# Two placement changes in a fused two-block transformer kernel: when GpSimd norms the residual stream, and when a mixer's convolution rows are turned

## The chip, the cores and the metric

The kernel runs on one core of one Trainium2 chip. The metric is the device time of one execution in microseconds (us), median over runs. A change below about 0.2% of it (3.3 us) can't be told from none.

## The reference

The input is a sequence of 256 tokens with 1024 features, in float32. Two blocks follow one another, each of two layers.

```python
def first_block(x, ...):
    for i in range(DEPTH):                       # 2 layers
        h = rmsnorm(x, norm_mix[i])
        x = x + (mixer_even if i % 2 == 0 else mixer_odd)(h, ...)
        x = x + ec_moe(rmsnorm(x, norm_ffn[i]), ...)      # 16 experts
    return rmsnorm(x, final_norm)                # gain "final_norm"

def second_block(x, ...):
    h = x
    for layer in range(DEPTH):                   # 2 layers
        h = h + 0.5 * _swiglu(_rmsnorm(h, norm_ffn1[layer]), ...)   # 1024 -> 2816 -> 1024
        hn = _rmsnorm(h, norm_mix[layer])
        h = h + (_attn_conv_mixer if layer % 2 == 0 else _recurrent_mixer)(hn, ...)
        h = h + 0.5 * _swiglu(_rmsnorm(h, norm_ffn2[layer]), ...)
    return _rmsnorm(h, norm_final)

def _attn_conv_mixer(h, ...):                    # "the third mixer"
    ...
    attn = _swa_sink_attention(q, k, v, sinks, rel_bias)
    glu = u[..., o3:o4] * jax.nn.sigmoid(u[..., o4:])
    c = jax.nn.silu(_layernorm(_causal_depthwise_conv(glu, conv_w, conv_b), ln_g, ln_b))
    return jnp.concatenate([attn, c], axis=-1) @ w_out
```

Between the blocks stands `rmsnorm(x, final_norm)`. Its result is both the input of the first feed-forward of the second block and the residual stream that this feed-forward is added to.

## The kernel before

The program is written engine by engine, and every engine works through its own list in the order in which the code issues it. Semaphores are the only thing that ties the engines together, so the order around the change is the order of the code.

**Units.** Weights come from memory in slots of 128 x 4096 float32 (2048 KB) into a ring of six. A slot holds four units of 128 x 1024. Each unit is split in two before TensorE uses it: ScalarE copies it, rounded, into `unit_hi` (`split_high`, L548), and VectorE subtracts that from the original into `unit_lo` (`split_low`, L553). There are four buffers of either, so the high part of unit u is written once TensorE has used unit u-4. Activations are split in the same way (`hT_hi` and `cat_lo`, `near_both`, `act_hi` and `act_lo`), and TensorE computes high x high, low x high and high x low.

**Feed-forward `ffn0`.** It is worked off in 22 tiles of 128 hidden features. A tile f has a gate unit, an up unit and a down unit. TensorE computes gate and up (L2004, L2005 with the high part, L2008 with the low one; in the first tile L2019, L2020, L2026), VectorE scales them by the row norms (`scaled`, L2145), ScalarE takes the silu (L2115), and VectorE multiplies (`product`: L2154, L2155, and L2157, which raises the semaphore `ffn_act`). TensorE then runs the down unit of tile f (L2082) behind gate and up of tile f+1, so product f has the time of two hidden matmul groups to be ready. On VectorE a tile is: low part of the next gate unit, scale gate, low part of the next up unit, scale up, product, low part of the down unit.

**Norming the stream.** The second block's first feed-forward reads the rows of x as they came out of the experts; the norm between the blocks is folded into its scales. The stream itself must still be normed before `ffn0` is added to it. That is `restore_pool` on GpSimd: two multiplications of 128 x 1024 by the gain row (L1115) and two by the rows' scale (L1118). It waits for the scale (`power_out`) and for the last transposes that read the raw x (`turned`). VectorE waits for its signal (`x_ready` 3) only after the 22nd tile. GpSimd has nothing else to do until the next norm.

**The third mixer's output projection `s_out`.** The concatenated row has 1024 features: the first 512 from attention, the last 512 from the convolution. The projection has eight units (c, j), c the half of the output columns and j the pair of 128-feature blocks of the input, in the order of `MIXED_UNITS`: (0,0), (0,1), (1,0), (1,1), (0,2), (0,3), (1,2), (1,3). The first four need attention alone, the others the convolution rows. The convolution, done by VectorE, ends about when attention does. Its layer norm's statistics follow (`norm_conv`), and VectorE signals the normed rows with `ln_done` (L2408). TensorE turns these rows, 8 transposes in two groups of four (`turn_pe(pe, "cat_s")`, L430), ScalarE takes the silu out of the two banks (`conv_silu`, L2318) and makes the high part (L2323), and VectorE makes the low part (`conv_low`, L2415). Unit (0,2), the fifth, waits for that. A table load for silu stands ahead of L2318 on ScalarE.

Numbering the units 0 to 7, TensorE's order before is units 0, 1, 2, 3, turn, units 4 to 7 (L2273 with the high parts, L2279 with the low ones). ScalarE splits units 0 to 3, runs `conv_silu`, then splits 4 to 7 and two units of the next feed-forward. VectorE splits units 0 and 1 inside `norm_conv`, then 2 and 3, then makes the low parts of the rows, then splits 4 to 7. The eighth unit is interleaved with the residual's additions (L787) and the next norm.

Of the kernel before, what the change touches and what calls it, by code (L numbers as in the profile page):

```python
# [70 lines left out]
def build(nc, stream, ahead, params, consts, buckets, final_rows, x_in, out):  # L71
    ctx = ExitStack()
    with ctx:
# [3 lines left out]
        def sem(name):  # L77
            return ctx.enter_context(nc.semaphore(name))
# [21 lines left out]
        def pc(name):  # L100
            return par[:, PCOL[name][0]:PCOL[name][1]]
# [102 lines left out]
        ffn_act = sem("ffn_act")  # L204
# [24 lines left out]
        def ge(eng, s, v):  # L229

            if v > 0:
                eng.wait_ge(s, v)
# [8 lines left out]
        def used(eng, n):  # L241

            eng.wait_ge(slot_used[n % RING], n // RING + 1)
# [176 lines left out]
        def turn_pe(pe, name, lo=0, hi=None):  # L420
            first, end = TURN_AT[name]
            for g in range(first + lo, end if hi is None else first + hi):
                if g >= 4:
                    pe.wait_ge(*TURN_DONE[g - 4])
                for src, at, rows, cols in TURNS[g][0]:
                    out = bank[g % 4][0:rows, at:at + cols]
                    if name == "s1" and g == end - 1:
                        last = nc.tensor.matmul(out, src, flip, start=True, stop=True)
                    else:
                        last = nc.tensor.transpose(out, src, ident)  # L430
                last.then_inc(turned, 1)
# [98 lines left out]
        def high_buf(name, u):  # L530
            if name in ("r_in", "r_out"):
                return rec_units[(u + (16 if name == "r_out" else 0)) % 3][0][:, :]
            return unit_hi[:, buffer(name, u), :]

        def low_buf(name, u):
            if name in ("r_in", "r_out"):
                return rec_units[(u + (16 if name == "r_out" else 0)) % 3][1][:, :]
            return unit_lo[:, buffer(name, u), :]
# [440 lines left out]
        rows, rows_sq = W[:, 0:D], W[:, 2048:2048 + D]  # L979
        x_sq = [W[:, 1024:1536], W[:, 1536:2048], W[:, 4096:4608], W[:, 4608:5120]]  # L980
        ZX, ZZ, ZM, ZR = 80, 84, 88, 104

        def quarter_ready(eng, p, i):

            eng.wait_ge(*(PARTS[p][i] if i < 3 else X_SOURCE[p]))
# [125 lines left out]
        def restore_pool(pool):  # L1111
            pool.wait_ge(power_out, POWERS["f0"] + 1)
            pool.wait_ge(turned, TURN_AT["n4"][1])
            for t in range(NT):
                nc.gpsimd.tensor_tensor(x[:, t, :], x[:, t, :], rows, ALU.mult).then_inc(weighted, 1)  # L1115
            pool.wait_ge(weighted, NT)
            for t in range(NT):
                last = nc.gpsimd.tensor_scalar(x[:, t, :], x[:, t, :], stat[:, ZR + t:ZR + t + 1], None, ALU.mult)  # L1118
            last.then_inc(x_ready, 1)
# [1075 lines left out]


        conv_bank = [bank[0], bank[1]]
        convw = pc("convw").rearrange("p (c j) -> p c j", c=4)

        OPS = [(c, j) for c in range(4) for j in range(KW + 1)]  # L2200
# [2 lines left out]
        def s_mix_pe(pe):  # L2203
# [41 lines left out]
            for u, (c, j) in enumerate(MIXED_UNITS):  # L2245
                high = high_buf("s_out", u).rearrange("p (k c) -> p k c", k=2)
                low = low_buf("s_out", u).rearrange("p (k c) -> p k c", k=2)
                if u == 4:
                    pe.wait_ge(ln_done, 1)
                    turn_pe(pe, "cat_s")  # L2250
                if c == 0:
                    left_ready(pe, "s_out", j)
                if j == 0:
                    for t in range(NT):
                        ge(pe, proj_free[t], freed(first + c - 2, t))
                high_ready(pe, "s_out", u)
                if (c, j) == MIXED_UNITS[-1]:
                    low_ready(pe, "s_out", u)
                    for t in range(NT):
                        for kk in range(2):  # L2260
                            for left, right in ((hT_hi, high), (cat_lo, high), (hT_hi, low)):
                                mm = nc.tensor.matmul(proj_bank(first + c, t)[:, :], left[:, 2 * j + kk, t * P:(t + 1) * P],
                                                      right[:, kk, :], start=False, stop=(kk == 1 and right is low),
                                                      skip_group_check=True)
                        mm.then_inc(unit_used if t else tail_done, 1)
                        if t == 0:
                            raw_turn_pe(pe, "n6", 0)
                            raw_turn_pe(pe, "n6", 1)
                    break
                for kk in range(2):  # L2270
                    for t in range(NT):
                        for left in (hT_hi, cat_lo):
                            nc.tensor.matmul(proj_bank(first + c, t)[:, :], left[:, 2 * j + kk, t * P:(t + 1) * P],  # L2273
                                             high[:, kk, :], start=(j == 0 and kk == 0 and left is hT_hi), stop=False,
                                             skip_group_check=True)
                low_ready(pe, "s_out", u)
                for kk in range(2):
                    for t in range(NT):
                        mm = nc.tensor.matmul(proj_bank(first + c, t)[:, :], hT_hi[:, 2 * j + kk, t * P:(t + 1) * P],  # L2279
                                              low[:, kk, :], start=False, stop=(j == 3 and kk == 1), skip_group_check=True)  # L2280
                mm.then_inc(unit_used, 1)

        def s_mix_act(act):
            n0 = START["s_in"]

            def gate(c):
                if c % 2 == 0:
                    act.wait_ge(wide_done, 1 + c // 2)
                else:
                    used(act, n0 + c // 2)  # L2290
                ge(act, wide_dve, c - 1)
                nc.scalar.activation(gate_s[:, c % 2, :], bank[4 + c][:, T:2 * T], ACT.Sigmoid).then_inc(wide_act, 1)

            gate(0)
            act.wait_ge(spread_ready, 1)
            act.dma_start(spread.ap(), spread_sb).then_inc(spread_out, 16)
            gate(1)
            act.wait_ge(spread_out, 16)
            for t in range(NT):
                src = bass.AP(tensor=spread, offset=1 + P * t, ap=[[1, P], [SPAN, S_HEADS], [1, T]])  # L2300
                act.dma_start(bias_s[:, :, t * T:(t + 1) * T], src).then_inc(rows_in, 16)
            gate(2)
            gate(3)
            for m in range(*PROJ_AT["s_in"]):
                for t in range(NT):
                    proj_copy_one(act, m, t, (uS[:, t, 0:512], uS[:, t, 512:768])[m - PROJ_AT["s_in"][0]], scalar=True)
            act.wait_ge(v_turned, 1)
            nc.scalar.activation(vS[:, :, :].rearrange("p a b -> p (a b)"), bank[7][:, 0:T], ACT.Copy).then_inc(v_out, 1)
            turn_evac(act, 0, "s1")
            attend_act(act, "s")  # L2310

            def conv_silu():
                for j in (2, 3):
                    g = TURN_AT["cat_s"][0] + j - 2
                    act.wait_ge(turned, g + 1)
                    for kk in range(2):
                        c = 2 * j - 4 + kk
                        last = nc.scalar.activation(silu_s[:, c, :], bank[g % 4][:, kk * T:(kk + 1) * T], ACT.Silu,  # L2318
                                                    bias=pc("lnb")[:, c:c + 1], scale=pc("lng")[:, c:c + 1])
                    last.then_inc(silu_done, 1)  # L2320
                for j in (2, 3):
                    act.wait_ge(silu_done, j - 1)
                    nc.scalar.activation(hT_hi[:, 2 * j:2 * j + 2, :], silu_s[:, 2 * j - 4:2 * j - 2, :],  # L2323
                                         ACT.Copy).then_inc(turn_hi, 1)

            for u in range(4):
                split_high(act, "s_out", u)
            conv_silu()
            for u in range(4, 8):
                split_high(act, "s_out", u)  # L2330
            for u in range(EARLY):
                split_high(act, "ffn1", u)

        def s_mix_dve(v):
# [48 lines left out]
            between = [107, 114, 120, 126, 128]  # L2383
            attend_dve(v, "s", lambda i: taps(between[i], between[i + 1]), first=lambda: taps(103, between[0]))
            norm_conv(v)
            for u in range(2, 4):
                split_low(v, "s_out", u)
            for j in (2, 3):
                conv_low(v, j)
            for u in range(4, 8):  # L2390
                split_low(v, "s_out", u)
            ahead_low(v, "ffn1")
            residual_add(v, "s_out")
# [579 lines left out]
```

## Time and profile before

| | us |
|---|---|
| median of 3 runs | 1632.93 (1632.87 to 1633.9) |
| span of the profiled execution | 1628.0 |
| TensorE matmul busy in the span | 1435.8 |
| VectorE busy | 942.5 |
| ScalarE busy | 614.5 |
| GpSimd busy | 41.6 |

The profiled execution is given by its span, from the first to the last instruction; no time of its own is listed beside it. The median lies 4.9 us above the span, for what is around the instructions. Times in the rows are positions in the span. PE is TensorE's matmul, PEld its weight load, DVE VectorE, ACT ScalarE, POOL GpSimd. A timeline row has the start, the duration, the engine, the line, the operation, output<-inputs, the shape, and in brackets the idle time ahead of it and who ended it.

### The profile page before, as it was taken

To read this page: it belongs to the slowest core of one execution; us is meant where nothing else is said; L and a number is where in the kernel's file an instruction comes from. 1 tells how busy PE (TensorE), PEld (TensorE's weight loads), DVE (VectorE), ACT (ScalarE), POOL (GpSimd) and SP (SyncE) were. 2 spreads that over 40 slices of the span, in tenths; PEclk is the share of its full clock that TensorE was granted. 3 is DMA by queue.
4 is the path that set the end of the run, shared out by engine and by line. 5 is a ranking of instruction groups with operands and counts; after the bars stand their busy time and mean duration, and the time that the engine had idled before them with its cause. 6 is when DMAs were issued, how large, how long until landed. Compare 5 with 4: busy or idle time off the path is not lost.

```text
span 1628.0 us, 29234 instructions
## 1 busy us (share of the span) xinstructions
PE 1435.8 (88%) x12036; PEld 1223.6 (75%) x12036; DVE 942.5 (58%) x1802; ACT 614.5 (38%) x1033; POOL 41.6 (3%) x45
## 2 busy tenths in 40 slices
PE   8988866688988676799999789999999999899998
PEld 6766433266664332599997469999999998799998
DVE  5675211166751111666667867666766668776666
ACT  5471101044711010444432354444544436654443
POOL 1000000001000000300000000000000000000000
PEclk9998988898989878999999989999999999999999
DMA  9936999996379999955464325455555552455510
GB/s 388 376 129 277 407 428 428 426 426 268 149 296 415 428 429 428 421 211 205 169 227 138 143 104 182 182 206 186 184 202 204 191 222 104 171 215 197 206 52 27
DMA packets 33071, 408.94 MB, mean 251 GB/s; under 512 B 3616, under 2 KB 5792, under 8 KB 8656
## 3 DMA queue, kind: packets, MB, share of 16 engines
q1 hardware_dynamic: 30528, 404.34, 62.7%
q10 hardware_dynamic: 2448, 3.24, 0.6%
q8 instruction: 71, 1.16, 0.3%
q14 instruction: 24, 0.20, 0.0%
HBM read 406.50 MB, written 1.06 MB: 250 GB/s over the span
## 4 chain that ended last, share of the span: by engine, by line
PE 72%; DMA 15%; DVE 8%; ACT 4%; issue 1%; SPq 0%; POOL 0%; POOLq 0%; DVEq 0%; ACTq 0%
PE bank L2082 15%; DMA ring<-stream 14%; PE bank L2004 9%; PE bank L2005 9%; PE bank L2008 9%; PE bank L694 4%; PE bank L1747 3%; PE bank L1779 2%; PE bank L1665 2%; PE bank L700 2%; PE bank L635 2%; PE bank L2214 2%; PE bank L662 1%; DVE unit_lo L553 1%; PE bank L1182 1%
## 5 line engine op out<-in xcount | busy, mean ns | idle before, releaser
L548 ACT ACTIVATE unit_hi<-ring 128x1024 fp32r<-128x1024 f32 x324 | 340.8, 1062 | 417.3 <-PE bank L2008 233.6
L553 DVE TENSOR_TENSOR unit_lo<-ring,unit_hi 128x1024 fp32r<-128x1024 f32 x324 | 394.2, 1225 | 156.8 <-ACT unit_hi L548 156.4
L2004 PE MATMUL bank<-near_both,unit_hi 128*128 128x256 f32 x1344 | 315.1, 277 | 0.0
L2005 PE MATMUL bank<-near_both,unit_hi 128*128 128x256 f32 x1344 | 314.2, 277 | 0.0
L2005 PEld LDWEIGHTS bank<-near_both,unit_hi 128*128 128x128 f32 x1344 | 252.7, 188 | 0.0
L2004 PEld LDWEIGHTS bank<-near_both,unit_hi 128*128 128x128 f32 x1344 | 252.5, 188 | 0.0
L1747 PE MATMUL bank<-ring,work 128*32 128x256 f32 x1792 | 129.7, 444 | 62.7 <-DMA ring<-stream 62.7
L2008 PE MATMUL bank<-near_both,unit_lo 128*128 128x256 f32 x1344 | 180.0, 276 | 0.6 <-DVE unit_lo L553 0.6
L2008 PEld LDWEIGHTS bank<-near_both,unit_lo 128*128 128x128 f32 x1344 | 164.9, 188 | 0.8 <-DVE unit_lo L553 0.8
L2082 PE MATMUL bank<-unit_hi,act_hi 128*128 128x256 f32 x672 | 162.9, 282 | 2.9 <-DVE act_lo L2157 2.9
L2082 PE MATMUL bank<-unit_hi,act_lo 128*128 128x256 f32 x672 | 163.2, 282 | 0.0
L1747 PEld LDWEIGHTS bank<-ring,work 128*32 128x32 f32 x1792 | 61.3, 124 | 129.8 <-DMA ring<-stream 81.4
L2082 PEld LDWEIGHTS bank<-unit_hi,act_hi 128*128 128x128 f32 x672 | 127.6, 190 | 3.1 <-issue 3.1
L1936 DVE TENSOR_TENSOR work<-work,bank 128x128 f32<-128x128 f32 x32 | 9.2, 287 | 206.8 <-ACT work L1836 206.8
L2082 PEld LDWEIGHTS bank<-unit_hi,act_lo 128*128 128x128 f32 x672 | 127.7, 190 | 0.0
L2145 DVE TENSOR_TENSOR work<-bank,xn 128x256 f32<-128x256 f32 x176 | 74.6, 424 | 74.7 <-PE bank L2008 68.0
L2082 PE MATMUL bank<-unit_lo,act_hi 128*128 128x256 f32 x672 | 93.3, 282 | 0.0
L1836 ACT ACTIVATE work<-bank 128x128 f32<-128x128 f32 x32 | 8.9, 277 | 211.1 <-PE bank L1747 211.1
L1779 PE MATMUL bank<-ring,work 128*32 128x256 f32 x960 | 67.9, 430 | 22.9 <-DMA ring<-stream 19.0
L2082 PEld LDWEIGHTS bank<-unit_lo,act_hi 128*128 128x128 f32 x672 | 85.7, 190 | 0.0
L1949 DVE COPY work<-bank 32x256 f32<-32x256 f32 x64 | 27.2, 425 | 82.2 <-PE bank L1779 81.7
L1846 ACT ACTIVATE work<-bank 32x256 f32<-32x256 f32 x64 | 23.9, 373 | 120.6 <-PE bank L1779 120.2
(347 smaller groups left out, 2024.7 us busy)
## 6 DMA issues: line engine op xcount, KB each, us to landing
ring<-stream SPq DMA_DIRECT2D x178, 2048.0 KB, 12.3
ring<-stream SPq DMA_DIRECT2D x12, 512.0 KB, 23.2
kept_slot<-ahead SPq DMA_DIRECT2D x2, 2048.0 KB, 27.8
ahead<-ahead SPq DMA_DIRECT2D x4, 1024.0 KB, 10.0
work<-ahead SPq DMA_DIRECT2D x2, 2048.0 KB, 8.6
ahead<-ahead SPq DMA_DIRECT2D x2, 2048.0 KB, 10.3
work<-ahead SPq DMA_DIRECT2D x2, 1280.0 KB, 5.8
work<-spread ACTq DMA_DIRECT2D x2, 1024.0 KB, 13.1
```

The lines of the kernel that those rows point to most:

```text
L548: nc.scalar.activation(high_buf(name, u), raw_unit(name, u), ACT.Copy).then_inc(hi_done, 1)
L553: low = nc.vector.tensor_tensor(low_buf(name, u), raw_unit(name, u), high_buf(name, u).bitcast(F32), ALU.subtract)
L635: mm = nc.tensor.matmul(proj_bank(m, t)[:, 0:width], lhs(k, t), rhs(k), start=(k == 0), stop=(k == tiles - 1))
L694: nc.tensor.matmul(proj_bank(m, t)[:, 0:width], left[:, 2 * j + kk, t * P:(t + 1) * P], high[:, kk, 0:width], start=(j == 0 and kk == 0 an ...
L700: mm = nc.tensor.matmul(proj_bank(m, t)[:, 0:width], left_hi[:, 2 * j + kk, t * P:(t + 1) * P], low[:, kk, 0:width], start=False, stop=(j ...
L1747: mm = nc.tensor.matmul(bank[4 + e % 2][32 * j:32 * j + 32, 0:256], hcur[:, 4 * half + kk, e * CAP:(e + 1) * CAP], w[:, kk, :, j * P:(j + ...
L1779: mm = nc.tensor.matmul(bank[7][32 * i:32 * i + 32, 0:256], actT_e[:, e % 2, j * CAP:(j + 1) * CAP], w[:, j, i * 256:(i + 1) * 256], start ...
L2004: nc.tensor.matmul(out, high[:, k, :], near(near_hi, k), start=(k == 0), stop=False)
L2005: nc.tensor.matmul(out, high[:, k, :], near(near_lo, k), start=False, stop=False)
L2008: mm = nc.tensor.matmul(out, low[:, k, :], near(near_hi, k), start=False, stop=(k == KD - 1))
L2082: return nc.tensor.matmul(bank[2 * t + c // 512][:, c % 512:c % 512 + DOWN], left[:, f % 2, t * P:(t + 1) * P], right[:, c:c + DOWN], star ...
L2145: nc.vector.tensor_tensor(out[:, f % 2, :], hidden_bank(f, which)[:, 0:T], row_scale, ALU.mult).then_inc(ffn_scaled, 1)
```

## The change

It has two parts that don't touch each other. In `ffn0`, GpSimd waits for one thing more before it norms the stream: four raises of `ffn_act`, that is the products of the first four tiles. In the third mixer, TensorE turns the convolution rows ahead of unit 3 and not behind it, ScalarE splits units 4 and 5 as well before the silu, and VectorE splits unit 4 as well before it makes the rows' low parts. No instruction that computes is added or removed.

```diff
@@ double_norm / restore_pool
+        RESTORE_AFTER = 4
...
         def restore_pool(pool):
             pool.wait_ge(power_out, POWERS["f0"] + 1)
             pool.wait_ge(turned, TURN_AT["n4"][1])
+            pool.wait_ge(ffn_act, RESTORE_AFTER)
             for t in range(NT):
@@ s_mix_pe
+        CONV_AFTER = 6
...
             for u, (c, j) in enumerate(MIXED_UNITS):
...
-                if u == 4:
+                if u == 3:
                     pe.wait_ge(ln_done, 1)
                     turn_pe(pe, "cat_s")
@@ s_mix_act
-            for u in range(4):
+            for u in range(CONV_AFTER):
                 split_high(act, "s_out", u)
             conv_silu()
-            for u in range(4, 8):
+            for u in range(CONV_AFTER, 8):
                 split_high(act, "s_out", u)
@@ s_mix_dve
             norm_conv(v)
-            for u in range(2, 4):
+            for u in range(2, CONV_AFTER - 1):
                 split_low(v, "s_out", u)
             for j in (2, 3):
                 conv_low(v, j)
-            for u in range(4, 8):
+            for u in range(CONV_AFTER - 1, 8):
                 split_low(v, "s_out", u)
```

Lines of the changed kernel are numbered one to three higher from here on (L2318 becomes L2321, L2273 becomes L2276). GpSimd's list at `restore_pool`, before:

```order
L886 TENSOR_TENSOR stat<-stat,con 128x4 [waits power_in]
L1115 TENSOR_TENSOR x<-x,work 128x1024 [waits turned,power_out]
L1115 TENSOR_TENSOR x<-x,work 128x1024
L1118 ISA
L1118 TENSOR_SCALAR x<-x,stat 128x1024 [waits weighted]
```

and now:

```order
L886 TENSOR_TENSOR stat<-stat,con 128x4 [waits power_in]
L1117 TENSOR_TENSOR x<-x,work 128x1024 [waits ffn_act,turned,power_out]
L1117 TENSOR_TENSOR x<-x,work 128x1024
L1120 ISA
L1120 TENSOR_SCALAR x<-x,stat 128x1024 [waits weighted]
```

The list is the same but for the third semaphore on the first multiplication.

TensorE's list in `s_out`, before, from the last matmul with unit 3's high part (bank4 and bank6 are unit 3's output) to the first of unit 4 (bank5); bank3 and bank0 take the turned rows:

```order
L2273 MATMUL bank6<-unit_hi_55,cat_lo_51 128x512
L2279 MATMUL bank4<-unit_lo_56,hT_hi_49 128x512 [waits slot_used1]
L2279 MATMUL bank6<-unit_lo_56,hT_hi_49 128x512
L2279 MATMUL bank4<-unit_lo_56,hT_hi_49 128x512
L2279 MATMUL bank6<-unit_lo_56,hT_hi_49 128x512
L430 MATMUL bank3<-con,cat 128x128 [waits turn_out_dve,ln_done]
L430 MATMUL bank3<-con,cat 128x128 x3
L430 MATMUL bank0<-con,cat 128x128 [waits turn_out_act]
L430 MATMUL bank0<-con,cat 128x128 x3
L2273 MATMUL bank5<-unit_hi_55,hT_hi_49 128x512 [waits hi_done,turn_lo]
```

and now, from the end of unit 2 to the first of unit 3 and then the first of unit 4:

```order
L2282 MATMUL bank6<-unit_lo_56,hT_hi_49 128x512
L430 MATMUL bank3<-con,cat 128x128 [waits turn_out_dve,ln_done]
L430 MATMUL bank3<-con,cat 128x128 x3
L430 MATMUL bank0<-con,cat 128x128 [waits turn_out_act]
L430 MATMUL bank0<-con,cat 128x128 x3
L2276 MATMUL bank4<-unit_hi_55,hT_hi_49 128x512 [waits hi_done]
...
L2282 MATMUL bank4<-unit_lo_56,hT_hi_49 128x512 [waits slot_used1]
...
L2282 MATMUL bank6<-unit_lo_56,hT_hi_49 128x512
L2276 MATMUL bank5<-unit_hi_55,hT_hi_49 128x512 [waits hi_done,turn_lo]
```

The eight transposes have moved ahead of unit 3's twelve matmuls, which now stand between them and the wait for `turn_lo`.

ScalarE's list at the same place, before:

```order
L548 ACTIVATE unit_hi_55<-ring 128x1024 [waits slot_in1]
L548 ACTIVATE unit_hi_55<-ring 128x1024 x3
L2318 ACT_TABLE_LOAD
L2318 ACTIVATE work<-bank3,par 128x256 [waits turned]
L2318 ACTIVATE work<-bank3,par 128x256
L2318 ACTIVATE work<-bank0,par 128x256 [waits turned]
L2318 ACTIVATE work<-bank0,par 128x256
L2323 ACTIVATE hT_hi_49<-work 128x512 [waits silu_done] x2
L548 ACTIVATE unit_hi_55<-ring 128x1024 [waits unit_used,slot_in2]
L548 ACTIVATE unit_hi_55<-ring 128x1024 [waits unit_used] x3
```

and now:

```order
L548 ACTIVATE unit_hi_55<-ring 128x1024 [waits slot_in1]
L548 ACTIVATE unit_hi_55<-ring 128x1024 x3
L548 ACTIVATE unit_hi_55<-ring 128x1024 [waits unit_used,slot_in2]
L548 ACTIVATE unit_hi_55<-ring 128x1024 [waits unit_used]
L2321 ACT_TABLE_LOAD
L2321 ACTIVATE work<-bank3,par 128x256 [waits turned]
L2321 ACTIVATE work<-bank3,par 128x256
L2321 ACTIVATE work<-bank0,par 128x256 [waits turned]
L2321 ACTIVATE work<-bank0,par 128x256
L2326 ACTIVATE hT_hi_49<-work 128x512 [waits silu_done] x2
L548 ACTIVATE unit_hi_55<-ring 128x1024 [waits unit_used] x2
```

The splits of units 4 and 5, with their waits for TensorE, stand ahead of the table load and the silu.

## Rows read from the trace of the kernel before

**Rows 1.** The page, busy time of each engine

```profile
PE 1435.8 (88%) x12036; PEld 1223.6 (75%) x12036; DVE 942.5 (58%) x1802; ACT 614.5 (38%) x1033; POOL 41.6 (3%) x45
```

**Rows 2.** Timeline of TensorE, `ffn0`, end of tile 1's up and tile 0's down

```profile
681.01 1.20 PE L2008 MATMUL bank<-near_both,unit_lo 128*128 128x256 f32 x8 [0.57 <-DVE unit_lo L553]
685.13 0.36 PE L2082 MATMUL bank<-unit_hi,act_hi 128*128 128x256 f32 x1 [2.92 <-DVE act_lo L2157]
```

**Rows 3.** Timeline of GpSimd

```profile
677.49 5.71 POOL L1115 TENSOR_TENSOR x<-x,work 128x1024 f32<-128x1024 f32 x2
683.29 6.68 POOL L1118 TENSOR_SCALAR x<-x,stat 128x1024 f32<-128x1024 f32 x2
```

**Rows 4.** Timeline of VectorE in the same stretch

```profile
679.36 1.60 DVE L553 TENSOR_TENSOR unit_lo<-ring,unit_hi 128x1024 fp32r<-128x1024 f32 x1
...
681.33 2.15 DVE L2154 TENSOR_TENSOR work<-work 128x256 f32<-128x256 f32 x1
...
683.85 1.14 DVE L2157 TENSOR_TENSOR act_lo<-work,act_hi 128x256 fp32r<-128x256 f32 x1
...
687.52 1.80 DVE L553 TENSOR_TENSOR unit_lo<-ring,unit_hi 128x1024 fp32r<-128x1024 f32 x1
```

**Rows 5.** Timeline of VectorE in tile 3, GpSimd idle

```profile
699.16 1.23 DVE L553 TENSOR_TENSOR unit_lo<-ring,unit_hi 128x1024 fp32r<-128x1024 f32 x1 [1.00 <-ACT unit_hi L548]
...
704.08 0.42 DVE L2154 TENSOR_TENSOR work<-work 128x256 f32<-128x256 f32 x1
...
704.87 0.43 DVE L2157 TENSOR_TENSOR act_lo<-work,act_hi 128x256 fp32r<-128x256 f32 x1
```

**Rows 6.** Chain that ended last, `ffn0`: start, us, what; down units, tiles 0 and 3

```profile
685.13 4.61 PE bank L2082 x24
...
711.78 2.83 PE bank L2082 x24
```

**Rows 7.** Stretches: length, busy (instructions), granted clock share, DMA share, GB/s

```profile
685.10:689.70 4.60, 4.57 (x26) 0.63 1.02 435
...
961.68:966.25 4.57, 4.57 (x13) 0.63 0.02 4
966.25:968.99 2.74, 2.74 (x13) 1.00 0.62 132
```

**Rows 8.** Stretches, busy of all engines (PE, PEld, DVE, ACT, POOL) ahead of clock

```profile
681.00:682.00 1.00, 0.99 (x8) 0.99 (x8) 0.96 (x2) 1.00 (x2) 1.00 (x1) 1.00 1.04 442
...
690.00:700.00 10.00, 10.00 (x89) 10.00 (x89) 8.29 (x13) 4.41 (x5) 0.00 (x0) 1.00 0.78 298
```

**Rows 9.** Chain that ended last, `s_out`, units 1 and 2, turn, silu

```profile
950.79 0.91 PE bank L2279 x4
...
953.51 0.91 PE bank L2279 x4
...
957.14 0.45 PE bank L430 x4
...
957.62 1.93 ACT work L2318 x4
```

**Rows 10.** Timeline of TensorE, turn and unit 4

```profile
956.98 1.04 PE L430 MATMUL bank<-con,cat 128*128 128x128 f32 x8
961.68 0.47 PE L2273 MATMUL bank<-unit_hi,hT_hi 128*128 128x512 f32 x1 [3.66 <-ACT unit_hi L548]
```

**Rows 11.** Timeline of ScalarE, `s_out`

```profile
966.34 1.06 ACT L548 ACTIVATE unit_hi<-ring 128x1024 fp32r<-128x1024 f32 x1 [1.97 <-PE bank L2279]
```

**Rows 12.** Timeline of VectorE, `s_out`

```profile
951.57 2.35 DVE L553 TENSOR_TENSOR unit_lo<-ring,unit_hi 128x1024 fp32r<-128x1024 f32 x2
960.10 1.29 DVE L2415 TENSOR_TENSOR cat_lo<-work,hT_hi 128x512 fp32r<-128x512 f32 x2 [6.18 <-ACT hT_hi L2323]
```

**Rows 13.** Timeline of ScalarE, a table load with work directly behind it

```profile
1399.86 1.28 ACT L2490 ACT_TABLE_LOAD   x1
1401.15 1.58 ACT L2490 ACTIVATE work<-bank 128x512 f32<-128x512 f32 x3
```

## The prediction

> **What bounds the kernel.** I read the page first: TensorE is busy for 1435.8 of 1628.0 us, VectorE for 942.5, GpSimd for 41.6 [rows 1]. So a microsecond is won where TensorE stands still or runs at the lower clock, and only if another engine's lateness is the reason. Then I asked for TensorE's waits in the two places the change touches, followed the chain that ended last through them, and laid the timelines of the engines behind TensorE's wait side by side.
>
> In `ffn0` TensorE waits twice. The low part of tile 1's up unit holds it for 0.57 us, and the product of tile 0 for 2.92 us [rows 2]. From then on the chain is TensorE alone: this was its only long wait in `ffn0`. GpSimd norms the stream at just that time, from 677.49 to 689.97 [rows 3], and VectorE's instructions beside it are long: L553 takes 1.60 us, L2154 2.15, L2157 1.14, a later L553 1.80 [rows 4]. The same instructions in tile 3, with GpSimd idle, take 1.23, 0.42 and 0.43 [rows 5]. VectorE loses 0.37 + 1.73 + 0.71 = 2.81 us ahead of the product that TensorE waits for, and 0.57 behind it, 3.4 in all. After the wait the granted clock falls from the 2.4 GHz level to that of 1.2 GHz for most of tile 0's down unit (0.63 over 4.6 us) [rows 7], and these 24 matmuls take 4.61 us of the chain where tile 3's take 2.83 [rows 6]: 1.78 us more.
>
> In `s_out` TensorE has no work between the turn of the convolution rows and unit 4. It starts the turn at 957.14 on the chain, the first group is out after 0.45, ScalarE's silu runs from 957.62 for 1.93 [rows 9], VectorE's low part starts at 960.10 [rows 12], and unit 4 at 961.68, after 3.66 us idle [rows 10]. The last to release it is ScalarE's high part of unit 4, which is queued behind the silu. Again the clock falls: unit 4 takes 4.57 us at a granted 0.63, and unit 5, the same work, 2.74 at 1.00 [rows 7].
>
> **Part one, the stream.** It removes nothing from TensorE's list. At the old place VectorE's four long instructions become short. L553 at 679.36 ends 0.37 earlier, so TensorE's low matmuls start at 680.64 and it is through with tile 1's hidden part at 681.84 instead of 682.21 (685.13 less 2.92). The product is ready 2.81 earlier, so the down unit starts at 685.13 - 2.81 = 682.32. The wait is 0.5 us, like the 0.57 ahead of it, after which the clock stayed at 1.00 [rows 8]. I take it that it does not fall here either. Gain: 2.81 + 1.78 = 4.59 us. If the clock falls anyway, the gain is 2.8.
>
> At the new place the four instructions start with product 3, that is at 705.30 less 4.6, about 700.7, and run 12.5 us beside tiles 4 and 5. Their cover is TensorE's lead over VectorE. Product 3 ended at 705.30 (704.87 + 0.43) [rows 5], and TensorE came to that tile's down unit at 711.78 [rows 6]: 6.5 us. The low part of the next gate unit, ended at 700.39, has a wider margin still, since TensorE first works through the up unit, a down unit and the next high part. VectorE is busy 8.29 of 10 us from 690 to 700, ScalarE 4.41 [rows 8], so it regains lateness too. Nothing is queued behind the new wait on GpSimd before the norm behind `ffn0`, and VectorE wants the stream after tile 22 only. The price from below is nothing, the loss measured at the old place is 3.4, and both are under 6.5, so I cost it at nothing. The bound from above is that VectorE stands for the whole 12.5 us: then TensorE waits 12.5 - 6.5 = 6.0 and the clock costs 1.8 again, and part one ends at 4.6 - 7.8 = -3.2.
>
> The Trainium skill has a rule on this ("SBUF — State Buffer", Who interferes with whom): a VectorE instruction with two SBUF inputs and a GpSimd instruction that reads SBUF exclude one another, and the later one stands still until the other has finished. The rows at the old place look like that: only instructions with two SBUF inputs are long, and L2154 ends at 683.48, just behind the end of L1115 at 683.20. Read at its worst, the rule gives the bound just named, since each GpSimd instruction can hold VectorE for its whole length; it is the rule that speaks against this part.
>
> **Part two, the turn.** TensorE ends unit 2 at 953.51 + 0.91 = 954.42 and starts the turn there, 2.72 us before the old 957.14. The rows are normed in time: VectorE's splits behind L2408 start at 951.57 [rows 12], 2.8 us before. TensorE's sum of turn and unit 3 is unchanged, so it reaches unit 4 at 956.98 + 1.04 = 958.02 as before [rows 10].
>
> ScalarE first has to be free for the silu. Its split of unit 5 waits for unit 1 on TensorE, used at 950.79 + 0.91 = 951.70 [rows 9], plus the 0.09 that L548 took behind unit 4 (966.25 to 966.34) [rows 7, 11], plus 1.06: 952.85. Unit 4's split is done before that. The table load now comes here and takes 1.28, with 0.01 to the next instruction [rows 13]: 954.14. The first turned bank is there at 954.42 + 0.45 + 0.03 = 954.90, so ScalarE is free 0.76 us before. Silu, high part and the first low part then follow as before, 2.72 earlier: VectorE starts L2415 at 957.38, and its first half, 0.65 us, is out at 958.03. VectorE is free for it, having split units 2, 3 and now 4 from 951.57 to 955.1. Unit 4's parts are both ready. TensorE starts unit 4 at 958.07, 0.05 us after it could, and without an idle stretch the clock stays. Gain: 961.68 - 958.07 = 3.61, and 4.57 - 2.74 = 1.83 from the clock, together 5.44 us. Without the clock's part it is 3.6.
>
> Units 5 to 7 keep this. VectorE splits unit 5 from 958.7 to 959.9, and TensorE wants its low part at 958.07 + 2.74 + 1.81 = 962.6; units 6 and 7 are split by 962.2. The next feed-forward's first two units wait for units 4 and 5 on TensorE and move with them, as do the residual's additions behind them. So all that follows starts 5.4 us earlier.
>
> The Trainium skill ("ScalarE: Activation LUTs", What ACT_TABLE_LOAD costs) gives 1.28 us for a table load and 1.38 more for a drain. Rows 13 show 1.29 from the load to the next instruction's start; by the page's 2.66 the silu would start at 955.5 and part two give 4.8.
>
> **The sum.** 4.59 + 5.44 = 10.0 us. Behind both places TensorE's chain has no wait on a transfer: the ring is filled ahead, DMA's share falls to 0.78 in 690 to 700 while TensorE runs on [rows 8], so an earlier start is kept to the end. The span goes from 1628.0 to 1618.0, and with the 4.9 us by which the median stands above the span, the time from 1632.93 to 1622.9 us.
>
> **The rivals.**
> A: a clock fall stays. It follows a long idle stretch in both places of before, and I have no row of this case with a wait of 0.5 us that was followed by one. But TensorE waits 0.57 and then 0.5 close together. One fall kept: 1624.7; both: 1626.5. Chance 0.10.
> B: GpSimd's work in the loop costs TensorE time. For it: the losses of rows 4. Against it: 3.4 us of loss under 6.5 of margin. Its bound, the page's rule at its worst, is 1632.9 - 10.0 + 7.8 = 1630.7. Chance 0.06, mostly below that.
> C: the silu or unit 4 is late. The slack is 0.76 on ScalarE and none on VectorE's low part; a late start by 0.6 to 1.5 us gives 1623.5 to 1624.4, and one of 3.6, which leaves the wait where it was, 1628.3. Chance 0.12.
> D: slower. VectorE and GpSimd take turns at the port for tile after tile, so that each VectorE instruction with two SBUF inputs (six in a tile) loses the 1.73 us that L2154 lost: 10.4 us a tile, less the 1.7 that it is idle in 10 us [rows 8]. It decides when VectorE falls behind by more than 6.5 + 10.0 - 1.8 + 3.3 = 18 us, which is just over two tiles; three tiles make 26.1 late and 19.6 of wait, a total of 1632.9 - 10.0 + 19.6 + 1.8 = 1644.3. Against it: the same 12.5 us of GpSimd cost VectorE 3.4 at the old place. Chance 0.02.
> E: neither part does what it says, because other engines set the same waits at the same times: 1632.9. Every link of both chains is in the rows, so 0.02.
>
> **The numbers.** The forecast has 0.68, and its own error is some 1.5 us, from where clock changes elsewhere fall. The range from 1621.0 to 1627.0 holds it, A, and most of C. What a measurement can tell from no change is about 0.2%, 3.3 us, so faster means below 1629.6: the forecast, A, C and most of B, 0.94; same 0.04; slower 0.02.
>
> **What the profile after would show.** VectorE's L553, L2156 and L2159 of tile 0 at 1.2, 0.4 and 0.4 us; TensorE's wait for tile 0's product at 0.5, its down unit at 2.8. GpSimd's two rows start near 700.7, some VectorE instructions beside them are long, and TensorE has no wait in the loop. In `s_out`, all 4.6 earlier: turn ahead of unit 3, table load ahead of the silu by under a microsecond, no wait above 0.2 ahead of unit 4, granted clock 1.00 through unit 5. Wrong would make me: a TensorE wait on `act_lo` in tiles 4 to 6, a clock of 0.5 at 682 to 686, or a wait on `cat_lo` or ScalarE ahead of unit 4.

## The result, and the profile after

| | before | after |
|---|---|---|
| median of 6 runs, us | 1633.19 (1629.88 to 1638.09) | 1620.96 (1615.59 to 1626.94) |
| span of the profiled execution | 1628.0 | 1616.7 |

The ratio is 0.9931 with a 95% interval of 0.9911 to 0.9951, that is 8 to 14.5 us less. Forecast were 10.0 less and 1622.9 us, in a range from 1621.0 to 1627.0. The median of 1620.96 is the lower end of that range, to the rounding, and the two medians differ by 12.2 us. One execution of `e2_turn_only` below took 4918.5 us, three times the others, and stands in neither its time nor its ratio.

Single runs of one kernel scatter by some 10 us. In the traces most of that lies ahead of `ffn0`, where no two kernels differ. So the parts are measured inside the traces, between GpSimd's power instructions L886, of which one stands ahead of each norm. Timeline of GpSimd, kernel after:

```profile
673.20 1.92 POOL L886 TENSOR_TENSOR stat<-stat,con 128x4 f32<-128x4 f32 x1 [65.57 <-DVE stat L1109]
698.51 6.57 POOL L1117 TENSOR_TENSOR x<-x,work 128x1024 f32<-128x1024 f32 x2 [23.40 <-DVE act_lo L2159]
705.18 7.94 POOL L1120 TENSOR_SCALAR x<-x,stat 128x1024 f32<-128x1024 f32 x2
852.13 1.66 POOL L886 TENSOR_TENSOR stat<-stat,con 128x1 f32<-128x1 f32 x2 [139.02 <-ACT stat L866]
941.34 1.92 POOL L886 TENSOR_TENSOR stat<-stat,con 128x4 f32<-128x4 f32 x1 [87.55 <-DVE stat L2407]
965.73 0.70 POOL L886 TENSOR_TENSOR stat<-stat,con 128x2 f32<-128x2 f32 x1 [22.46 <-DVE stat L1064]
```

and the same instructions of the kernel before:

```profile
675.49 1.92 POOL L886 TENSOR_TENSOR stat<-stat,con 128x4 f32<-128x4 f32 x1 [64.44 <-DVE stat L1108]
859.09 1.65 POOL L886 TENSOR_TENSOR stat<-stat,con 128x1 f32<-128x1 f32 x2 [169.12 <-ACT stat L866]
948.16 1.92 POOL L886 TENSOR_TENSOR stat<-stat,con 128x4 f32<-128x4 f32 x1 [87.42 <-DVE stat L2404]
977.63 0.70 POOL L886 TENSOR_TENSOR stat<-stat,con 128x2 f32<-128x2 f32 x1 [27.55 <-DVE stat L1063]
```

A distance is the time from the start of one L886 to the start of the next. The first distance, over `ffn0`, went from 183.60 to 178.93: 4.67 less. The second, from the convolution's layer norm to the next norm, went from 29.47 to 24.39: 5.08 less. Together that is 9.75. Of the 11.3 by which the span is shorter, 2.29 were there before `ffn0` began (675.49 against 673.20), where nothing was changed, and 0.7 were lost again elsewhere. The stretch between the two distances, which the change doesn't touch, is 89.21 and was 89.07; in the other kernels it is up to 91.60.

In `ffn0`, the timelines of TensorE and VectorE that answer to [rows 2] and [rows 4]:

```profile
678.04 1.20 PE L2010 MATMUL bank<-near_both,unit_lo 128*128 128x256 f32 x8 [0.23 <-DVE unit_lo L553]
679.72 0.35 PE L2084 MATMUL bank<-unit_hi,act_hi 128*128 128x256 f32 x1 [0.49 <-DVE act_lo L2159]
```

```profile
676.77 1.22 DVE L553 TENSOR_TENSOR unit_lo<-ring,unit_hi 128x1024 fp32r<-128x1024 f32 x1
...
678.35 0.42 DVE L2156 TENSOR_TENSOR work<-work 128x256 f32<-128x256 f32 x1
...
679.15 0.42 DVE L2159 TENSOR_TENSOR act_lo<-work,act_hi 128x256 fp32r<-128x256 f32 x1
...
700.49 2.32 DVE L553 TENSOR_TENSOR unit_lo<-ring,unit_hi 128x1024 fp32r<-128x1024 f32 x1 [1.01 <-ACT unit_hi L548]
...
703.23 2.93 DVE L553 TENSOR_TENSOR unit_lo<-ring,unit_hi 128x1024 fp32r<-128x1024 f32 x1
...
706.62 0.80 DVE L2156 TENSOR_TENSOR work<-work 128x256 f32<-128x256 f32 x1
```

The first three are short, and TensorE's wait of 2.92 has become 0.49. The last three are long beside GpSimd's new place. They lost 1.1 + 1.7 + 0.4 = 3.2 us there, against 3.4 at the old place, and TensorE has no wait at all from 690 on.

In `s_out`, the chain that ended last, kernel after, answering to [rows 9, 10], and ScalarE's timeline:

```profile
947.60 0.45 PE bank L430 x4
...
948.07 1.93 ACT work L2321 x4
950.01 0.53 ACT hT_hi L2326
...
950.56 0.70 DVE cat_lo L2418
...
951.30 2.14 PE bank L2276 x8
953.44 0.92 PE bank L2282 x4
```

```profile
944.91 1.07 ACT L548 ACTIVATE unit_hi<-ring 128x1024 fp32r<-128x1024 f32 x1 [1.60 <-PE bank L2282]
945.99 1.28 ACT L2321 ACT_TABLE_LOAD   x1
948.07 1.93 ACT L2321 ACTIVATE work<-bank,par 128x256 f32<-128x256 f32 x4 [0.80 <-PE bank L430]
```

The table load is through 0.80 us before the turned bank. Unit 4 is released by the low part of the rows and no longer by its own split. From the start of the turn to unit 4 it is 3.70 us. TensorE's last matmul of unit 3 ends at 951.21, so it stands idle for 0.09 us where it stood for 3.66. The granted clock is 1.00 through both places:

```profile
679.70:682.60 2.90, 2.88 (x24) 1.00 0.99 415
951.30:954.36 3.06, 3.06 (x13) 1.00 0.84 353
```

### The profile page after: what moved, and what is told of

It reads as the page before. It is cut to its first block, busy times and chain, and to the rows that moved or that the text cites. A ratio compares the mean times of both kernels' runs of the same rounds, so it can differ in the third digit from the quotient of the medians.

```text
span 1616.7 us, 29234 instructions
## 1 busy us (share of the span) xinstructions
PE 1434.6 (89%) x12036; PEld 1219.9 (75%) x12036; DVE 941.7 (58%) x1802; ACT 614.4 (38%) x1033; POOL 43.7 (3%) x45
## 4 chain that ended last, share of the span: by engine, by line
PE 71%; DMA 14%; DVE 9%; ACT 4%; issue 1%; SPq 0%; POOL 0%; POOLq 0%; DVEq 0%; ACTq 0%
PE bank L2084 15%; DMA ring<-stream 14%; PE bank L2006 9%; PE bank L2007 9%; PE bank L2010 9%; PE bank L694 4%; PE bank L1749 3%; PE bank L1781 2%; PE bank L1667 2%; PE bank L700 2%; PE bank L635 2%; PE bank L2217 2%; PE bank L662 1%; DVE unit_lo L553 1%; PE bank L1801 1%
## 5 line engine op out<-in xcount | busy, mean ns | idle before, releaser
L553 DVE TENSOR_TENSOR unit_lo<-ring,unit_hi 128x1024 fp32r<-128x1024 f32 x324 | 396.1, 1231 | 153.5 <-ACT unit_hi L548 153.2
L1749 PE MATMUL bank<-ring,work 128*32 128x256 f32 x1792 | 131.8, 450 | 61.5 <-DMA ring<-stream 61.5
L2147 DVE TENSOR_TENSOR work<-bank,xn 128x256 f32<-128x256 f32 x176 | 74.7, 424 | 72.6 <-PE bank L2010 66.3
L1781 PE MATMUL bank<-ring,work 128*32 128x256 f32 x960 | 69.1, 435 | 19.3 <-DMA ring<-stream 14.4
L694 PE MATMUL bank<-unit_hi,hT_hi 128*128 128x512 f32 (+2 forms) x176 | 64.5, 372 | 5.2 <-ACT unit_hi L548 5.2
## 6 DMA issues: line engine op xcount, KB each, us to landing
ring<-stream SPq DMA_DIRECT2D x178, 2048.0 KB, 12.4
```

The costliest lines, as they stand in the source:

```text
L553: low = nc.vector.tensor_tensor(low_buf(name, u), raw_unit(name, u), high_buf(name, u).bitcast(F32), ALU.subtract)
L694: nc.tensor.matmul(proj_bank(m, t)[:, 0:width], left[:, 2 * j + kk, t * P:(t + 1) * P], high[:, kk, 0:width], start=(j == 0 and kk == 0 an ...
L1749: mm = nc.tensor.matmul(bank[4 + e % 2][32 * j:32 * j + 32, 0:256], hcur[:, 4 * half + kk, e * CAP:(e + 1) * CAP], w[:, kk, :, j * P:(j + ...
L1781: mm = nc.tensor.matmul(bank[7][32 * i:32 * i + 32, 0:256], actT_e[:, e % 2, j * CAP:(j + 1) * CAP], w[:, j, i * 256:(i + 1) * 256], start ...
L2147: nc.vector.tensor_tensor(out[:, f % 2, :], hidden_bank(f, which)[:, 0:T], row_scale, ALU.mult).then_inc(ffn_scaled, 1)
```

## The experiments

All distances below are read from L886 as above, "first" over `ffn0` and "second" over `s_out`.

**Each part alone.** `e1_stream_only` is the changed kernel with the third mixer as before:

```diff
-                if u == 3:
+                if u == 4:
-            for u in range(CONV_AFTER):       # ScalarE; also range(CONV_AFTER, 8)
+            for u in range(4):                #          range(4, 8)
-            for u in range(2, CONV_AFTER - 1):   # VectorE; also range(CONV_AFTER - 1, 8)
+            for u in range(2, 4):                #          range(4, 8)
```

> Part one alone: GpSimd waits for four products, the third mixer as before. Measured inside the trace, to leave out what happens ahead of it: from GpSimd's power instruction L886 ahead of ffn0 to the one behind it took 183.60 us before and 178.93 with both parts; from L886 of the convolution's layer norm to the next one took 29.47 and 24.39. Theory: the first distance is 178.9 to 179.1, the second 29.4 to 29.5, and the time 4.6 us below the kernel before. Rival (the parts lean on one another, the gain of the first stretch being lost or made later): the first distance above 180 or the second below 29.

Measured: first 178.92, second 29.48. The time was 1628.67 against 1631.15, ratio 0.9984 (0.9964 to 1.0005), so by its time alone this part can't be told from nothing.

`e2_turn_only` takes out `pool.wait_ge(ffn_act, RESTORE_AFTER)` and leaves the rest.

> Part two alone: turn, splits and low parts as changed, GpSimd norms the stream as before. Theory: first distance 183.6, second 24.4 (the predicted 5.44 less would be 24.0), time 5.1 us below before. Together with part one alone the gains add to 9.7. Rival: the parts are not independent, and the two gains add to under 8 or over 12.

Measured: first 183.57, second 24.36, time 1623.34, ratio 0.9951 (0.9931 to 0.9971). Each distance moved with its own part and by nothing else, to 0.1 us. The parts add up.

**Taking part two apart.** Both kernels have the stream as before. In `e3_turn_no_splits` only TensorE's turn is moved, in `e4_splits_no_turn` only the splits:

```diff
 e3:  if u == 3:   ScalarE range(4), range(4, 8)   VectorE range(2, 4), range(4, 8)
 e4:  if u == 4:   ScalarE range(6), range(6, 8)   VectorE range(2, 5), range(5, 8)
```

> TensorE's turn ahead of unit 3, but ScalarE splits units 4 and 5 behind the silu and VectorE unit 4 behind the low parts, as before. GpSimd as before. Theory: unit 4's high part is then made behind the high part of the rows, one L548 of 1.06 later, so TensorE starts unit 4 about 0.75 us later than with the splits ahead; TensorE's wait there is about 1.0 us and the clock stays: second distance 25.2. If a wait of 1 us is enough for the clock to fall, 27.0. Rival (the turn is worth nothing by itself, unit 4 was held by its split): 29.5.

> The splits ahead of the silu as changed, but TensorE turns the rows behind unit 3 as before. GpSimd as before. Theory: unit 4 is then released by VectorE's low part, about 0.9 us ahead of ScalarE's split that released it before, and the clock still falls: second distance 28.6. Rival (the splits are what was worth something): 25 or less.

Measured: second 25.17 and 28.41, ratios 0.9962 (0.9942 to 0.9982) and 0.9982 (0.9962 to 1.0002). The chains show the two releases. With the turn alone, ScalarE's split of unit 4 behind the high part:

```profile
960.39 0.64 ACT hT_hi L2325
961.03 0.95 ACT unit_hi L548
...
962.12 2.08 PE bank L2275 x8
```

With the splits alone, VectorE's low part, and behind it a unit whose first matmuls run at the low clock:

```profile
962.58 0.70 DVE cat_lo L2417
...
963.32 3.44 PE bank L2275 x8
```

The turn alone is worth 4.3 us of the 5.08, the splits 0.8 on top of it, and 1.1 by themselves (0.2 of it because unit 4 took 4.36 for 4.57). A wait of 0.94 us ahead of unit 4 in `e3` did not lower the clock; 2.8 us in `e4` did.

In `e4`, `ffn0` is that of the kernel before, and yet its first distance is 184.63, where the kernel before, `e2` and `e3` have 183.60, 183.57 and 183.78. The wait for tile 0's product is the same, 2.93, but the clock came back later, and the down unit took 5.46 where it took 4.61:

```profile
684.05 5.46 PE bank L2083 x24
```

So a fall of the clock behind one and the same wait doesn't always cost the same.

**The clock's share.** `e7_fill_waits` is the kernel before with matmuls in the two waits:

```diff
+                if name == "ffn0" and f == 0:          # down(), ahead of the wait for ffn_act
+                    for _ in range(24):
+                        nc.tensor.matmul(bank[3][:, 0:T], high[:, 0:P], near(near_hi, 0), start=True, stop=True, ...)
...
                     turn_pe(pe, "cat_s")
+                    for _ in range(15):
+                        nc.tensor.matmul(bank[1][:, :], hT_hi[:, 0, 0:P], hT_hi[:, 0:2, :]..., start=True, stop=True, ...)
```

> The kernel before, with both waits left in place but filled: 24 more matmuls of 128x256 into a bank not in use ahead of the wait for product 0 (2.8 us), and 15 of 128x512 behind the turn of the convolution rows (3.4 us). Nothing reads their results. It tests the clock's share of the gain. Theory (the clock falls because TensorE stands still there): it stays at 1.00 in both, tile 0's down unit takes 2.83 and not 4.61, unit 4 2.74 and not 4.57; first distance 183.6 - 1.8 = 181.8, second 29.47 - 1.8 = 27.7. Rival (the clock falls at these places for another reason): 183.6 and 29.5.

Measured: first 182.04, second 27.87, that is 1.56 and 1.60 less. The chain:

```profile
688.02 3.10 PE bank L2086 x24
```

```profile
963.25 2.06 PE bank L2280 x8
965.31 0.91 PE bank L2286 x4
```

The waited-for instructions came no earlier, TensorE only did not stand still, and the clock stayed at 1.00. So about a third of each part's gain is the clock, as this pair of traces has it. It is 0.2 less than I had put down, since tile 0's down unit takes 3.10 and unit 4 2.97, where later ones take 2.83 and 2.74, at the same granted clock. The fill ended 0.15 and 0.26 us too early, and the difference is in the first matmul behind that gap (last section).

**How far TensorE's lead covers.** `e5_restore_1` has `RESTORE_AFTER = 1`.

> The changed kernel, but GpSimd starts behind the product of the first tile, not of the fourth (RESTORE_AFTER = 1). It norms the stream beside tiles 1 and 2. In the changed kernel's trace product 1 was ready at 684.90 and TensorE came to it at 688.09, a lead of 3.2 us, where at the place of the change it is 6.5. The loss of VectorE there was about 3.2 us. Theory (the loss is hidden exactly as far as TensorE's lead reaches): product 1 or a low part ahead of it comes 0.3 to 2 us late for TensorE, the first distance is 179.2 to 181, and up to 1.8 more if the clock falls. Rival (any place behind the first product hides it): 178.9 and no wait. Rival (GpSimd's whole 12 to 15 us are the price): above 185.

Measured: first 180.87, which is 1.94 more than with four; 0.3 of that is TensorE's place at the start of the stretch, as the section on the prediction shows. TensorE again waits for a product, of tile 1, after VectorE's two low parts took 4.55 us for 2.35, the next one 3.10 for 1.22 and L2156 0.89 for 0.42. That is 4.5 us lost ahead of the product, more than the lead of 3.2:

```profile
675.48 4.55 DVE L553 TENSOR_TENSOR unit_lo<-ring,unit_hi 128x1024 fp32r<-128x1024 f32 x2
```

```profile
683.44 1.21 PE L2010 MATMUL bank<-near_both,unit_lo 128*128 128x256 f32 x8
685.49 0.38 PE L2084 MATMUL bank<-unit_hi,act_hi 128*128 128x256 f32 x1 [0.84 <-DVE act_lo L2159]
```

The clock stayed at 1.00. `e6_pool_busy` loads the loop instead:

```diff
             pool.wait_ge(weighted, NT)
+            for i in range(24):
+                nc.gpsimd.tensor_tensor(kept_slot[:, 2 * D:3 * D], kept_slot[:, 0:D], kept_slot[:, D:2 * D],
+                                        ALU.mult).then_inc(weighted, 1)
+                pool.wait_ge(weighted, NT + 1 + i)
```

> The changed kernel with 24 more multiplications of 128x1024 on GpSimd between the two by the gains and the two by the scale, on a buffer that is not in use, each waiting for the one before. Results are unchanged. GpSimd is then busy beside some eight tiles. Theory (the lock costs VectorE at the rate seen at the new place, 3.2 us in the 14.6 that GpSimd was busy, about 1.8 us a tile, less than the 2.5 that VectorE is idle in a tile): first distance stays 178.9, no wait of TensorE in the loop, though VectorE's instructions are long in every tile. Rival D of the prediction (VectorE and GpSimd take turns, every VectorE instruction with two SBUF inputs is held): VectorE needs over 10 us for a tile of 8.3, TensorE waits in each of them from the second or third on, first distance 190 or more.

Measured: first 211.58. This theory fell, and rival D's mechanism is real. With GpSimd never out of work, VectorE and GpSimd take strict turns: every VectorE instruction with two SBUF inputs waits for one of GpSimd's, and L2151, which reads PSUM, never does.

```profile
717.77 6.74 DVE L553 TENSOR_TENSOR unit_lo<-ring,unit_hi 128x1024 fp32r<-128x1024 f32 x2
724.43 0.41 DVE L2151 TENSOR_TENSOR work<-bank,xn 128x256 f32<-128x256 f32 x1
724.76 3.09 DVE L553 TENSOR_TENSOR unit_lo<-ring,unit_hi 128x1024 fp32r<-128x1024 f32 x1
727.78 0.41 DVE L2151 TENSOR_TENSOR work<-bank,xn 128x256 f32<-128x256 f32 x1
728.31 2.05 DVE L2160 TENSOR_TENSOR work<-work 128x256 f32<-128x256 f32 x1
730.28 2.55 DVE L2161 TENSOR_TENSOR act_hi<-work 128x256 fp32r<-128x256 f32 x1
732.87 2.45 DVE L2163 TENSOR_TENSOR act_lo<-work,act_hi 128x256 fp32r<-128x256 f32 x1
735.24 6.72 DVE L553 TENSOR_TENSOR unit_lo<-ring,unit_hi 128x1024 fp32r<-128x1024 f32 x2
```

From one tile's L553 to the next it is 17.5 us, where TensorE needs 8.3. GpSimd's 24 extra instructions took 69.87 us, 2.91 each, and six of them, one for each such VectorE instruction of a tile, make the 17.5. TensorE waited 22.5 us in the loop. The other 10 of the 32.65 more are the clock, granted at 0.82 to 0.84 from 720 to 780, and the start behind each wait; the two were not separated. `e10_pool_2` and `e11_pool_5` have 2 and 5 extra instructions in place of 24.

> The changed kernel with 2 more multiplications on GpSimd in place of the 24, to find where TensorE's lead ends. In the run with 24, VectorE's every instruction with two SBUF inputs waited for one of GpSimd's, a tile took 17.5 us, and TensorE first stood (0.72 us, then 1.23) when about three extra ones had passed. Theory (the lead of 6.5 us is the cover, not a rate): two extra ones cost nothing, first distance 178.9 to 179.2. Rival (the changed kernel sits on the edge already): above 180.

> The same with 5 more. Theory: past the edge. TensorE waits for product 4 and for a low part as in the run with 24, about 0.7 + 1.2, and 1 to 3 more behind them, with a clock fall if one wait is long: first distance 181 to 185. Rival (the loss in the run with 24 came only from its long duration): 178.9.

Measured: first 179.23 with two, with no wait of TensorE in the loop, and 182.86 with five. With five TensorE waits four times, the clock stays at 1.00, and the two longest waits are these:

```profile
723.11 0.38 PE L2088 MATMUL bank<-unit_hi,act_hi 128*128 128x256 f32 x1 [0.72 <-DVE act_lo L2163]
726.43 1.18 PE L2088 MATMUL bank<-unit_lo,act_hi 128*128 128x256 f32 x8 [1.22 <-DVE unit_lo L553]
```

**Nothing as cover.** `e8_restore_22` has `RESTORE_AFTER = 22`.

> The changed kernel, but GpSimd waits for all 22 products. It then works beside the last down unit and beside nothing. It measures what its four instructions take without VectorE's, and what the wait on the stream costs when nothing covers it. Theory (they hold the port for about 2.4 + 2.1 + 1.3 + 1.0 us by what they cost VectorE at the old place, and the longer spans of the rows were their own waiting): they take 7 to 9 us together, VectorE waits 4 to 6 for the stream, first distance 183 to 187 with a fall of the clock. Rival (they take the 12.4 us of the rows): first distance 188 or more.

Measured: first 188.04, at the rival's bound, though GpSimd took neither my 7 to 9 us nor the rival's 12.4, but 10.4:

```profile
856.16 4.72 POOL L1117 TENSOR_TENSOR x<-x,work 128x1024 f32<-128x1024 f32 x2 [172.81 <-DVE act_lo L2159]
860.98 5.67 POOL L1120 TENSOR_SCALAR x<-x,stat 128x1024 f32<-128x1024 f32 x2
```

VectorE's residual waited 10.69 us for L1120. GpSimd alone needs 10.4 us, and beside VectorE at the new place 14.5. So it is held up too.

**One unit further.** `e9_turn_ahead_2` has `if u == 2` on TensorE.

> The changed kernel with TensorE's turn one unit earlier still, ahead of unit 2. In the changed kernel TensorE stood 0.25 us ahead of unit 4 for the rows' low part, and the first matmuls behind a wait were 0.3 slower. ln_done is there at 944.83 of its trace and TensorE ends unit 1 at 944.87, so the turn starts with no wait to speak of. ScalarE is free for the silu 2.4 us behind that (split of unit 5, table load), which two units of TensorE cover. Theory: second distance 24.39 less 0.3 to 0.6, that is 23.8 to 24.1; first distance 178.9. Rival (the table load is now on the path, or the turn waits for ln_done): 24.4 or more.

Measured: second 24.19, first 179.22, time 1624.95 against 1633.5, ratio 0.9951 (0.9924 to 0.9978). The wait ahead of unit 4 is gone, but the distance fell by 0.20 only, less than expected. The rival was partly right: the turn now comes so soon that its first weight load waits for the normed rows:

```profile
PEld bank L430 <- DVE cat L2411: 0.4, 1, 0.4
```

That is no version that can be told from the changed kernel.

## Why the prediction was right

**Part one, 4.59 forecast, 4.67 measured.** The steps held one by one: VectorE's instructions at 1.22, 0.42, 0.42; the wait 0.49 for 0.5; no fall of the clock. Two small errors cancel. The down unit behind the wait took 3.07 where I had put 2.83, as in `e7`, so the clock's share is 1.5 and not 1.78. And TensorE happened to stand 0.3 us nearer to the norm's statistic when the stretch began (L2147's first start is 3.22 us behind L886 and was 3.52), which is not the change's doing, and whose cause is open: `e4`, with the stream as before, has 3.22 as well, and `e9` and `e10`, with it changed, have 3.52 and first distances of 179.22 and 179.23. Like for like the part is therefore worth 183.60 - 179.22 = 4.4, and that the measured 4.67 came so close to 4.59 is in part luck. `e1` gives the part by itself.

**The new place, forecast at nothing.** Right: no wait, 3.2 us of loss for the 3.4 that the old place had. The cover is the lead of 6.5 us, as the prediction said, and `e5`, `e10` and `e11` bracket it. With a lead of 3.2 the same work costs 1.9 (1.65 like for like), with 6.5 two further GpSimd instructions are free, and five cost 3.9. GpSimd was there for 14.6 us and not for the 12.5 forecast, which the lead covered too. What I made of it afterwards, in the expectation for `e6`, was wrong: the loss is no rate to be set against VectorE's idle time. It comes by turns, one GpSimd instruction for each VectorE instruction with two SBUF inputs. Rival D in the prediction had priced just that, at 10.4 us a tile and 8.7 net of VectorE's idle time; the 17.5 us of a tile less the some 5.6 that VectorE works in one when undisturbed are 11.9, and less TensorE's 8.3 they are 9.2. The section on the kernel before says that semaphores alone tie the engines together; these turns are a second tie, and no semaphore shows it. D did not happen since GpSimd has four instructions there and not dozens.

The Trainium skill's rule ("SBUF — State Buffer", Who interferes with whom) agrees with `e6` in what blocks (L553 long, L2151 not) and in that VectorE waits for a whole GpSimd instruction each time. Its bound at the worst, rival B's 1630.7, was not reached: within GpSimd's 14.5 us VectorE lost 3.2. The two multiplications with two SBUF inputs took 2.8 of that. During the two by a scalar only L2156 was long, by 0.4, and the two L553 at 708.13 took 2.35 together as ever.

**Part two, 5.44 forecast, 5.08 measured.** The turn started 2.7 us sooner, the table load had 0.80 to spare for the 0.76 forecast, and the low part released unit 4. Of the 0.36 missing, 0.05 is the start of unit 4, 3.56 us sooner for 3.61, and 0.31 is again the start behind a wait: unit 4 took 3.06 for 2.74. TensorE's idle time ahead of it is 0.09, within the 0.2 that the prediction allowed. On the table load the measurement decides against the price of 2.66 in the Trainium skill ("ScalarE: Activation LUTs", What ACT_TABLE_LOAD costs): by it the silu would have been held 0.6 us, and it was not held; the load took 1.28 and ScalarE then waited 0.80.

**The sum, 10.0 forecast, 9.75 measured between the marks.** With the 0.3 of luck in part one taken off it is 9.45. The 0.6 then missing are in the unit behind the wait, which the prediction put at 2.83 and 2.74 us and which took 3.07 and 3.06. The 11.3 of the span and the ratio hold more than 9.75, and most of the difference lies ahead of `ffn0`. In the thirteen traces L886 ahead of `ffn0` starts between 668.9 and 682.5 us, without a pattern by kernel. The forecast range of 6 us was therefore about the effect. That the median of six runs came out at 1620.96, at its very edge, says nothing for or against the mechanism; for a median under such scatter the range was too narrow.

## What to carry to other kernels

Ask of background work on GpSimd not how long it takes but which lead covers it: count VectorE's instructions with two SBUF inputs beside it, give each the length of one GpSimd instruction, and compare the sum with the time between the moment a product is ready and the moment it is wanted. That sum is a bound, reached in `e6`, where GpSimd always had the next instruction ready; the four instructions of this kernel cost VectorE 3.2 to 5 us, by where they stood. At a hand-over between four engines, move the piece of independent work that the waiting engine has, here one unit, behind the hand-over's first step; moving only what the other engines do was worth a fifth of that. Where the scatter of a run is larger than the effect, measure the distance between two marks inside the trace, and look at the same distance in kernels that share its code: here the two distances agreed within 0.3 us where the code was the same, but for one that was off by 1.0, and the one between them did so only within 2.5.

## What was not expected of the hardware

A wait costs TensorE more than its idle time, at an unchanged granted clock of 1.00. Eight matmuls of 128x512 behind one took 2.14, 2.08 and 2.06 us in three kernels where they take 1.81, and 24 of 128x256 took 3.07 for 2.83. Nearly all of it is the first matmul. In the stream each starts before the one ahead of it has ended; the first behind a wait has nothing to overlap with and is itself longer. Timeline of TensorE, kernel after, behind the wait of 0.49:

```profile
679.72 0.35 PE L2084 MATMUL bank<-unit_hi,act_hi 128*128 128x256 f32 x1 [0.49 <-DVE act_lo L2159]
679.91 0.28 PE L2084 MATMUL bank<-unit_hi,act_lo 128*128 128x256 f32 x1
680.03 0.28 PE L2084 MATMUL bank<-unit_hi,act_hi 128*128 128x256 f32 x1
```

A matmul of the stream adds 0.12 us to the chain, and the first one adds its 0.35: 0.23 more, which is the 3.07 for 2.83. For 128x512 it is 0.47 to 0.50 against 0.23.

GpSimd's multiplication by a scalar takes 2.8 us alone, more than the 2.4 of the one with two inputs. At the new place two of them hardly held VectorE up, by 0.4 us, while GpSimd itself was lengthened by 2.3 us beside it. At the old place two of them cost VectorE 1.3 us (L2157 0.71 and L553 0.57 in [rows 4]). What decides between the two was not tested.
